# The pick grid of a routed expert layer: two of four column one-hots made on ScalarE, and four sets of one-hots instead of two

## The reference, cut to what matters

```python
for t in range(256):                       # tokens
    for k in range(128):                   # picks: 8 heads x 16
        grid[j[t, k], i[t, k], t] += weight[t, k]
y = (gelu(x @ U.T) * grid_of_the_token) @ V  # over all 16384 experts
```

## Time and profile before

| | us |
|---|---|
| median of 3 runs | 2251.58 (2249.17 to 2252.14) |
| the profiled execution | 2255.86 |
| its span, first to last instruction | 2254.1 |
| TensorE busy | 2112.1 (94%) |
| VectorE busy | 1494.1 (66%) |
| ScalarE busy | 1004.8 (45%) |
| GpSimd busy | 252.3 (11%) |
| mean granted TensorE clock, as a share of 2.4 GHz | 0.985 |

### The profile page before, as it was taken

How to read it: one execution, slowest core, us unless ns; L and a number is a source line. 1 busy time by engine, 2 the same in 40 slices (tenths; PEclk the granted TensorE clock), 3 DMA queues, 4 the chain that set the end, 5 groups by cost and what they waited for, 6 DMA issues and landing times.

```text
span 2254.1 us, 45848 instructions
## 1 busy us (share of the span) xinstructions
PE 2112.1 (94%) x15318; PEld 1945.4 (86%) x15318; DVE 1494.1 (66%) x3417; ACT 1004.8 (45%) x1976; POOL 252.3 (11%) x292
## 2 busy tenths in 40 slices
PE   8999999768999999999989999989998999999998
PEld 7758898657999999999988888889997878788998
DVE  5744696697667777777765366765655546676565
ACT  3331466323444444444455454544445545454444
POOL 0000399893000000000000000000000000000000
PEclk9989999999999999999999999999999999999999
DMA  7334555102558778788645522335553542244553
GB/s 292 112 113 153 220 168 164 60 0 97 183 183 263 256 257 262 256 271 261 228 141 161 182 95 90 127 128 185 183 185 124 166 152 94 85 151 140 186 186 112
DMA packets 103258, 376.14 MB, mean 167 GB/s; under 512 B 11472, under 2 KB 11728, under 8 KB 102880
## 3 DMA queue, kind: packets, MB, share of 16 engines
q1 hardware_dynamic: 88992, 323.86, 43.2%
q10 hardware_dynamic: 14144, 50.77, 6.9%
HBM read 373.54 MB, written 1.05 MB: 166 GB/s over the span
## 4 chain that ended last, share of the span: by engine, by line
PE 56%; issue 17%; DMA 10%; POOL 8%; DVE 4%; DVEq 3%; ACT 1%; ACTq 0%; POOLq 0%; PEldq 0%
PE bank L740 16%; PE bank L746 15%; PE bank L743 15%; DMA roots<-ada_dram 10%; POOL one_hots L1452 5%; POOL part_lo L1441 3%; DVEq L2002 1%; PE bank L878 1%; PE bank L964 1%; DVE part_lo L1728 1%; PE bank L918 1%; PE bank L923 1%; PE bank L925 1%; PE bank L920 1%; PE bank L842 1%
## 5 line engine op out<-in xcount | busy, mean ns | idle before, releaser
L1174 ACT ACTIVATE part_hi<-ring 128x512 fp32r<-128x512 f32 x1080 | 663.3, 627 | 528.7 <-PE bank L743 438.3
L740 PE MATMUL bank<-u_hi,part_hi 128*128 128x256 f32 (+1 forms) x2496 | 725.1, 290 | 51.6 <-DVE u_lo L1816 17.5
L746 PE MATMUL bank<-u_hi,part_lo 128*128 128x256 f32 (+1 forms) x2496 | 707.1, 283 | 0.0
L743 PE MATMUL bank<-u_lo,part_hi 128*128 128x256 f32 (+1 forms) x2496 | 705.6, 283 | 0.0
L1728 DVE TENSOR_TENSOR part_lo<-ring,part_hi 128x512 fp32r<-128x512 f32 x672 | 450.0, 689 | 201.1 <-ACT part_hi L1174 192.6
L740 PEld LDWEIGHTS bank<-u_hi,part_hi 128*128 128x128 f32 (+1 forms) x2496 | 474.2, 190 | 78.6 <-issue 33.0
L746 PEld LDWEIGHTS bank<-u_hi,part_lo 128*128 128x128 f32 (+1 forms) x2496 | 478.0, 192 | 0.5
L743 PEld LDWEIGHTS bank<-u_lo,part_hi 128*128 128x128 f32 (+1 forms) x2496 | 475.6, 191 | 1.0 <-issue 0.5
L740 PE MATMUL bank<-w_hi,part_hi 128*128 128x256 f32 x1376 | 391.1, 284 | 2.7 <-DVE part_lo L1728 1.8
L743 PE MATMUL bank<-w_lo,part_hi 128*128 128x256 f32 x1376 | 389.5, 283 | 0.0
L746 PE MATMUL bank<-w_hi,part_lo 128*128 128x256 f32 x1376 | 389.3, 283 | 0.0
(11 more groups left out here) (261 smaller groups left out, 2442.2 us busy)
## 6 DMA issues: line engine op xcount, KB each, us to landing
ring<-stream_dram SPq DMA_DIRECT2D x606, 512.0 KB, 3.3
roots<-ada_dram ACTq DMA_DIRECT2D x72, 512.0 KB, 4.6
arena<-ada_dram ACTq DMA_DIRECT2D x24, 512.0 KB, 8.0
xT<-x_dram SPq DMA_DIRECT2D x4, 256.0 KB, 5.4
arena<-mem_dram SPq DMA_DIRECT2D x1, 1024.0 KB, 9.5
arena<-keys_dram SPq DMA_DIRECT2D x1, 1024.0 KB, 5.4
out_dram<-uT SPq DMA_DIRECT2D x2, 512.0 KB, 2.6
cst<-consts_dram SPq DMA_DIRECT2D x1, 841.0 KB, 14.3
```

The lines of the kernel that those rows point to most:

```text
L740: m = pe.matmul(o, hi, u(cc), start=first, stop=False, **flags)
L743: m = pe.matmul(o, hi, l(cc), start=False, stop=False, **flags)
L746: m = pe.matmul(o, lo, u(cc), start=False, stop=last, **flags)
L1174: act.activation(part_hi[:, h % 4, 0:width], ring[:, n % RING, (h % 2) * width:(h % 2 + 1) * width], ACT.Copy).then_inc(hi_ready, 1)
```

## The change

It takes the column one-hot of one token from VectorE and of one more from GpSimd and gives these two to ScalarE. ScalarE has no comparison; it makes the distance |c - j| with Abs (the bias is a column of negated indices) and then Relu(1 - distance), which is 1 where the distance is 0 and 0 elsewhere. Both functions are exact for whole numbers. The Relu runs over the two tokens at once, behind a drain, since it reads what the Abs wrote. `pickT` gets a fourth row with the negated `j`, by one more copy out of the transposed bank.

The sets of one-hots become four, one per bank. They need 16 KB per partition and lie over the upper half of `part_hi`, all of `part_lo`, and `w_hi` and `w_lo`. `pg_full` starts at 4, and every engine may be four steps ahead of TensorE instead of two. VectorE's turn becomes: scale step s-4, then the rows of s. ScalarE's: the distances of s, the copy of step s-4, the drain, the Relu of s. TensorE waits for one more semaphore, ScalarE's `col_last`. The loops of VectorE and ScalarE have 15 turns, with the first four steps in front and the last four behind.

```diff
-        hots = nc.alloc_sbuf_tensor_at("one_hots", [P, 2, 8, P], F32, offset=lo_at)
+        hots = nc.alloc_sbuf_tensor_at("one_hots", [P, 4, 2, 4, P], F32, offset=lo_at - 4 * 1024)
...
-            pe.drain().then_inc(pg_full, 2)
+            pe.drain().then_inc(pg_full, 4)
...
+                    pe.wait_ge(col_last, it * 4 + (q + 1))
...
                     act.activation(pickT[:, 0:2, :].rearrange("p a b -> p (a b)"), bank[2][:, :], ACT.Copy)
+                    act.activation(pickT[:, 3, :], bank[2][:, S:2 * S], ACT.Copy, scale=-1.0)
...
+            def column_distance(q, it):
+                act.wait_ge(pg_full, it * 4 + (q + 1))
+                for t in (2, 3):
+                    act.activation(hot_j[:, q, t, :], cst[:, C_IOTA:C_IOTA + P], ACT.Abs,
+                                   bias=pickT[:, 3, bass.ds(it * 16 + q * 4 + t, 1)])
+
+            def last_columns(q):
+                last = hot_j[:, q, 2:4, :].rearrange("p a b -> p (a b)")
+                act.activation(last, last, ACT.Relu, scale=-1.0, bias=1.0).then_inc(col_last, 1)
...
+            for q in range(4):
+                column_distance(q, 0)
+            act.drain()
+            for q in range(4):
+                last_columns(q)
+            with act.Fori(1, S // 16) as it:
                 for q in range(4):
+                    column_distance(q, it)
+                    keep_grid(q, it - 1)
+                    act.drain()
+                    last_columns(q)
+            for q in range(4):
+                keep_grid(q, S // 16 - 1)
...
-                pool.wait_ge(pg_full, it * 2 + (q + 1))
-                for t in range(3):
+                pool.wait_ge(pg_full, it * 4 + (q + 1))
+                for t in (0, 1):
...
                 v.wait_ge(pg_full, it * 4 + (q + 1))
-                v.tensor_scalar(hot_j[:, (q % 2) * 4 + 3, :], cst[:, C_IOTA:C_IOTA + P],
-                                pickT[:, 1, bass.ds(it * 16 + q * 4 + 3, 1)], None, ALU.is_equal)
                 for t in range(4):
...
-            with v.Fori(0, S // 16 - 1) as it:
+            with v.Fori(1, S // 16) as it:
                 for q in range(4):
-                    row_hots(q + 2, it)
-                    scale_grid(q, it)
+                    scale_grid(q, it - 1)
+                    row_hots(q, it)
```

More of the change, by code:

```diff
@@ L791, in _ @@
                     pe.wait_ge(col_ready, it * 4 + (q + 1))
+                    pe.wait_ge(col_last, it * 4 + (q + 1))
                     for t in range(4):
-                        x = (q % 2) * 4 + t
-                        m = pe.matmul(bank[q][:, t * P:(t + 1) * P], hot_j[:, x, :], hot_i[:, x, :],
+                        m = pe.matmul(bank[q][:, t * P:(t + 1) * P], hot_j[:, q, t, :], hot_i[:, q, t, :],
                                       start=True, stop=True)
@@ L1203, in _, with keep_grid @@
             act.drain().then_inc(pg_out, 4)
-            with act.Fori(0, S // 16) as it:
-                for q in range(4):
[L1206 to L1209, removed]
+            def column_distance(q, it):
[6 more added lines that the diff above has]
+                act.activation(last, last, ACT.Relu, scale=-1.0, bias=1.0).then_inc(col_last, 1)
+            def keep_grid(q, it):
+                act.wait_ge(pg_scaled, it * 4 + (q + 1))
+                act.activation(G[:, AHEAD:NKEY, bass.ds(it * 16 + q * 4, 4)],
+                               bank[q][:, :].rearrange("p (t i) -> p i t", t=4)[:, AHEAD:NKEY, :],
+                               ACT.Copy).then_inc(pg_out, 1)
+            act.drain()
[5 more added lines that the diff above has]
+            with act.Fori(1, S // 16) as it:
+                for q in range(4):
+                    column_distance(q, it)
+                    keep_grid(q, it - 1)
+                    act.drain()
+                    last_columns(q)
+            for q in range(4):
+                keep_grid(q, S // 16 - 1)
             def fetch_ada(n, more):
@@ L1449, in column_hots @@
             def column_hots(q, it):
[L1450 to L1453 removed]
+                pool.wait_ge(pg_full, it * 4 + (q + 1))
+                for t in (0, 1):
+                    at = it * 16 + q * 4 + t
+                    m = pool.tensor_scalar(hot_j[:, q, t, :], cst[:, C_IOTA:C_IOTA + P], pickT[:, 1, at:at + 1], None,
+                                           ALU.is_equal)
                 m.then_inc(col_ready, 1)
             pool.wait_ge(turn_out, 1)
[L1457 to L1458 removed]
+            for it in range(S // 16):
+                for q in range(4):
                     column_hots(q, it)
@@ L1710, in _ @@
             v.wait_ge(gelu_done, AHEAD + 1)
-            row_hots(0, 0)
-            row_hots(1, 0)
-            with v.Fori(0, S // 16 - 1) as it:
+            for q in range(4):
+                row_hots(q, 0)
+            with v.Fori(1, S // 16) as it:
                 for q in range(4):
-                    row_hots(q + 2, it)
-                    scale_grid(q, it)
+                    scale_grid(q, it - 1)
+                    row_hots(q, it)
             for q in range(4):
-                if q < 2:
-                    row_hots(q + 2, S // 16 - 1)
                 scale_grid(q, S // 16 - 1)
```

11 lines of the change are left out of this document (6 added, 5 removed).

## The result

The changed kernel took 2236.83 us (median of 5 runs, 2232.09 to 2238.92) against 2251.58 us of the kernel before (5 runs beside them, 2246.91 to 2257.15): ratio 0.9925, interval 0.9906 to 0.9944. Timed again on another visit it took 2230.82 us (5 runs) against 2254.71 (9 runs): ratio 0.9888, interval 0.9870 to 0.9905. Faster, then: by 17 and 25 us by these ratios, which are estimated from the single runs, and by 14.8 and 23.9 by the medians alone. The forecast was 2232.9. The two intervals don't overlap, so something moves from one visit to the next that the runs of one visit don't show. The profiled executions took 2235.55 us and, in the second visit, 2231.01. Of the 4.5 us between them 4.3 lie ahead of the grid: the last expert matmul ends at 420.52 us in the one and at 416.24 in the other. Why is open.

A forecast was written before the change was run, and what follows sets the result against it. TensorE was busy 94%, but in the grid stage GpSimd's one-hots set 1.73 us a step. ScalarE's 1.45 would replace it, saving 19.2 us, 18.7 with loop turns: 2251.58 - 18.7 = 2232.9 us, range 2229.5 to 2239.5.

The forecast's parts named there:

- The bound before: Grid stage: GpSimd sets the 1.73 us step; VectorE, also full, would be a shade quicker alone at most.
- VectorE's term, 1.42: VectorE per grid step without its column one-hot: four row one-hots 1.15 plus scaling 0.27, 1.42 us.
- ScalarE's term, 1.45: ScalarE per grid step, two Abs, copy, drain and Relu: 0.31 + 0.31 + 0.44 + 0.08 + 0.31 = 1.45 us.
- The loop turn, 0.04: 0.04 us at each of 15 turns of ScalarE's grid loop, 0.6 us in all.
- The drain, 0.08: ScalarE's drain between copy and Relu in each grid step leaves 0.08 us; 0.05 less were it hidden.
- TensorE's wait and the clock: TensorE's waits name ScalarE's Relu; sign of being wrong: grid clock at 1.2 GHz beyond first 4 us, steps taking 1.78.
- The ring: Waits from ScalarE's pass s back to step s-4: 2.9 us round, 5.8 allowed with four sets; two would not fit.
- Case 1: Grid steps paced by ScalarE at 1.45 us, slightly less or more: gain 15 to 22 us, 83%.
- case 2: Grid pace above sum, by ScalarE's open queue work (1.60, total 2241.6) or VectorE slowed to 1.56 (2239.3 us); 12.5%.
- case 3: One function table load at each of 15 ScalarE grid turns, costing 19.2 us: 2252, no change; 2.5%.
- case 4: Abs or Relu absent from the table Gelu left: two ScalarE loads a grid step, 149 us more, 2382; 1%.
- Case 5: GpSimd and VectorE lock each other out in the grid: 2.57 us a step, 65 us more, 2298; 1%.

The follow-up runs named there:

- experiments 1 and 2: Changed kernel edited two ways: four sets with the old split of work, 2252.13 us; ScalarE taking only VectorE's column one-hot, GpSimd keeping three, 2259.65 us.
- experiment 8: Changed kernel with one column one-hot each on ScalarE and VectorE, two on GpSimd, GpSimd's left out after the first 32 steps: 2244.85 us.
- experiment 4: Changed kernel with two sets of one-hots instead of four, ScalarE's first four passes made one by one: 2222.96 us.
- experiments 6 and 7: First, experiment 6; second, that kernel with GpSimd's column one-hots left out after the first 32 steps: 2224.92 us.
- experiment 6: Changed kernel with a semaphore, raised by the second Abs and awaited by the Relu, in place of ScalarE's drain: 2226.66 us, again 2223.96 us.

## Why the prediction was right, and where its terms were off

- **The bound before.** "Two engines are full", with TensorE's wait put down to GpSimd: right that GpSimd bounds (experiments 1 and 2; its three one-hots are 3 x (11.56 - 0.6) / 19 = 1.731 us, not 1.732, and nothing hangs on that). But "VectorE would be a shade quicker alone at most" was wrong. Its six instructions come to 0.193 + 4 x 0.256 + 0.267 = 1.484 us, as experiment 8 shows without GpSimd. The 1.73 of the earlier trace rows were not its own work alone, and its 104.00 busy us of 104.00 hid 0.25 us of hold-up in each step. It is not waiting: VectorE's first one-hot of a step starts 0.49 us after TensorE has freed the set, and 0.19 us after where it does wait for that (experiment 4).
- **VectorE's term, 1.42.** Mis-sized, for the reason just given: it reads 1.15 and 0.27 off an engine paced by others. Its own pace is 1.29 (experiments 6 and 7). This did no harm, since ScalarE's term was above both. The remark that what the two engines do to each other is small, and is in my 1.42, was wrong: it was 0.25 us a step in the kernel before and 0.13 in experiment 8, and nothing to VectorE in experiments 6 and 7. In the bound of its own that the term should have given, none of it belonged.
- **ScalarE's term, 1.45.** 1.41 measured. The Abs took 0.29 where I had 0.31, the copy with its drain 0.50 where I had 0.52, the Relu 0.32 where I had 0.31. The Trainium skill, page "ScalarE: Activation LUTs", section "What ACT_TABLE_LOAD costs", would have given the Abs better than my row did: an estimate by its figures for a bias per partition and for the overlap of neighbours is 280 + 0.833 x 128 - 93 = 294 ns, and 0.292 us was measured.
- **The loop turn, 0.04.** Mis-sized: 0.13, or 15 x 0.13 = 2.0 us in all instead of 0.6. With 1.41 it gives 1.438 a step, where 1.45 and 0.01 of turns had been said.
- **The drain, 0.08.** The gap in the timeline is 0.09. In the sum that did no harm, since the copy stands there with its whole 0.44. What was mis-sized is what the drain costs in all, which the lower end of the range put at 0.05: copy to Relu takes 0.50 with it and 0.33 without, 0.17 more. With the semaphore the loop turn is hidden too, and the pace goes from 1.438 to 1.290; there VectorE's own pace takes over, so these 0.15 are a lower bound of what drain and turn cost ScalarE together.
- **TensorE's wait and the clock.** It does name ScalarE's Relu, though 21 of 51 waits are put down to VectorE, wrongly, as shown above. GpSimd's waits for TensorE are 0.23 to 0.36 us, where 0.3 was forecast. The granted clock was low for the first three microseconds of the grid in the first profile, as before, and for six in the second. That is beyond the four that the prediction named as a sign of being wrong, and it cost 0.6 us of stage.
- **Start and end.** 0.8 us later against one, and the last steps as before: right. The extra copy and the overlaid buffers cost nothing that shows: the Gelu at 420.55 still waits 0.59 us for TensorE.
- **The sum.** Stage 20.1 us shorter (19.5 in the second profile) against 18.7. The excess is the pace, 58 x (1.46 - 1.438) = 1.3 us. How near the whole time came is partly luck: by the medians the gain was 14.8 us in one visit and 23.9 in the other, on either side of the stage's 20, and the second is more than the 22.1 of the range's end. That spread lies in work that the change doesn't touch, and the prediction gave it no term.
- **The ring.** That two sets would not fit was right in sign: 3.0 us of stage with the drain, 6.0 with the semaphore.
- **The rivals.** Case 1 came true. Queue work in the open (case 2) was seen only as the loop turn. No table load falls in the stage (case 3, case 4). The Trainium skill, page "ScalarE: Activation LUTs", section "Table sets: the hidden batching unit", says that Abs, Relu and Copy are in every set. The stage agrees; the loop ahead of it, with seven loads at its copy, shows that a load can stand before a copy all the same. Case 5 was a lock for the whole length of an instruction. In experiment 6 VectorE's 1.29 us and GpSimd's two one-hots (1.155 by the 0.577 each of the kernel before) fit in a step of 1.29 instead of 2.45, so these instructions don't lock each other out for their whole length. The rule of the Trainium skill, page "SBUF — State Buffer", section "SBUF: two separate sides", that the prediction set beside this case, speaks of VectorE in a two-port mode or with two SBUF inputs. Whether VectorE ran in such a mode here no run shows. What remains is the hold-up of experiments 7 and 8.

## What to carry to other kernels

An engine busy 100% of a stretch may still have slack. Another engine's hold-up lengthens its records (VectorE's 0.33 us to 0.40 and more), and because neighbouring records overlap (by 0.1 us on ScalarE), a shorter wait leaves no idle time: ScalarE is busy 67.00 of 67.00 us in experiment 6 with an estimated 1.22 of every 1.29 as its own. An engine's own pace shows only where its partner is taken away. Here two one-sided edits (relieve the one, relieve the other) told the bound apart from the follower; the engine named as the releaser was right in most cases and wrong in 21 of 51. Between dependent instructions on one engine a semaphore can be much cheaper than a drain, because the gap seen beside the drain (0.09 us here) is the smaller part of its price (0.17). And where a long program has a stretch that waits for transfers, judge an edit by its own stage: here the part behind the grid took 1707.3 us in one execution of a kernel and 1716.8 in another.

## What the runs showed of the hardware that was not expected

- A drain between a copy and a Relu on ScalarE: gap 0.09 us, but 0.50 us from the copy's start to the Relu's where a semaphore leaves 0.33.
- GpSimd and VectorE, both on 128x128 comparisons from SBUF: VectorE 1.613 us for six instructions beside two of GpSimd's, 1.486 without; in another order of work VectorE 1.290 for five with and without, and GpSimd's 0.577 stretched to 0.646. In the kernel before VectorE took 1.731 for six beside three of GpSimd's, and GpSimd was not stretched.
- Behind a 128x128 comparison on VectorE with one scalar per partition the next instruction starts after 0.193 us, behind a comparison and multiplication with two after 0.256.
- A loop's turn on ScalarE: 0.13 us behind a body of 4 steps, 0.21 behind one of 12, and none to be seen once the drain is gone (pace 1.290 with VectorE as the bound).
